# First mixer of a two-model forward pass: projections cut into quarters between the steps of a blocked inverse, level masks on VectorE

## What is computed

```python
u = rms_norm(h, norm_mix[l]); proj = u @ w_in[l]
pool_out = pool_mixer(proj[..., :P], w_pool[l], pool_scale[l])
qkv = causal_conv_silu(proj[..., P:P + 3 * G], conv_w[l])
...
m = einsum('bhncd,bhnjd->bhncj', kb, kh) * decay_strict
sol = triangular_solve(eye(C) + m, [vh * beta, kb * exp(gcum)], lower=True)
...
h = h + concatenate([pool_out, gdn_out]) @ w_out[l]
h = h + square(relu(rms_norm(h, norm_mlp[l]) @ w_up[l])) @ w_down[l]
```

## Time and profile before

| what | us |
|---|---|
| median of the runs | 1176.15 |
| the profiled execution, its own time | 1177.17 |
| its span | 1175.4 |
| TensorE matmul busy | 1098.7 (93%) |
| VectorE / ScalarE / GpSimd busy | 720.2 / 550.3 / 46.5 |
| granted TensorE clock, mean | 0.975 |

### The profile page before, as it was taken

The page is one execution under the profiler, slowest core; times in us unless marked ns, Lnnn a source line. Parts: engine busy times, 40 slices in busy tenths (PEclk is TensorE's granted clock), DMA queues, the critical chain, the costliest instruction groups (busy, mean ns, idle before and its releaser), DMA issues.

```text
span 1175.4 us, 20755 instructions
## 1 busy us (share of the span) xinstructions
PE 1098.7 (93%) x8770; PEld 1064.4 (91%) x8770; DVE 720.2 (61%) x979; ACT 550.3 (47%) x656; POOL 46.5 (4%) x40
## 2 busy tenths in 40 slices
PE   5896688999999999999999999999699999999997
PEld 4886678999999879999999999998589899999997
...
GB/s 294 82 140 108 72 36 72 172 189 178 178 271 196 128 195 179 189 169 179 215 176 181 181 177 126 180 37 158 58 1 1 22 123 150 223 188 188 182 72 36
DMA packets 116960, 167.51 MB, mean 143 GB/s; under 512 B 5792, under 2 KB 97568, under 8 KB 116512
## 3 DMA queue, kind: packets, MB, share of 16 engines
...
...
## 4 chain that ended last, share of the span: by engine, by line
PE 80%; DVE 12%; issue 3%; ACT 3%; DMA 1%; POOL 0%; SPq 0%; DVEq 0%; ACTq 0%; POOLq 0%
PE banks L1874 22%; PE banks L1876 22%; PE banks L1875 22%; DVE sb_w_low L1145 2%; ACT sb_w_high L637 1%; PE banks L2302 1%; PE banks L2379 1%; DVE sb_arena L1215 1%; PE banks L2367 1%; DVE sb_arena L1735 1%; DMA sb_constants<-in_constants 1%; DVE sb_state L1732 1%; PE banks L2010 1%; PE banks L2017 1%; PE banks L2182 1%
## 5 line engine op out<-in xcount | busy, mean ns | idle before, releaser
L1145 DVE TENSOR_TENSOR sb_w_low<-sb_raw,sb_w_high 128x2048 fp32r<-128x2048 f32 x150 | 344.9, 2303 | 274.3 <-ACT sb_w_high L637 274.2
L1874 PE MATMUL banks<-sb_act_high,sb_w_low 128*128 128x256 f32 x1376 | 396.3, 288 | 16.4 <-DVE sb_arena L1204 5.9
L637 ACT ACTIVATE sb_w_high<-sb_raw 128x2048 fp32r<-128x2048 f32 x150 | 285.6, 1910 | 268.4 <-PE banks L1876 268.3
L1876 PE MATMUL banks<-sb_act_high,sb_w_high 128*128 128x256 f32 x1376 | 391.7, 285 | 0.0
L1875 PE MATMUL banks<-sb_act_low,sb_w_high 128*128 128x256 f32 x1376 | 389.1, 283 | 0.0
L1874 PEld LDWEIGHTS banks<-sb_act_high,sb_w_low 128*128 128x128 f32 x1376 | 261.7, 190 | 21.6 <-DVE sb_arena L1204 7.5
L1875 PEld LDWEIGHTS banks<-sb_act_low,sb_w_high 128*128 128x128 f32 x1376 | 264.2, 192 | 0.4 <-issue 0.2
L1876 PEld LDWEIGHTS banks<-sb_act_high,sb_w_high 128*128 128x128 f32 x1376 | 260.8, 190 | 0.0
L1874 PE MATMUL banks<-sb_hidden_high,sb_w_low 128*128 128x256 f32 x896 | 254.2, 284 | 0.6 <-DVE sb_hidden_low L1558 0.6
L1876 PE MATMUL banks<-sb_hidden_high,sb_w_high 128*128 128x256 f32 x896 | 253.5, 283 | 0.0
L1875 PE MATMUL banks<-sb_hidden_low,sb_w_high 128*128 128x256 f32 x896 | 251.3, 280 | 0.0
...
## 6 DMA issues: line engine op xcount, KB each, us to landing
...
```

The lines of the kernel that those rows point to most:

```text
L637: nc.scalar.activation(whi[s][:], raw[s][:], ACT.Copy).then_inc(hi_done, 1)
L1145: nc.vector.tensor_tensor(wlo[s][:], raw[s][:], f32(whi[s][:]), ALU.subtract).then_inc(lo_done, 1)
L1874: nc.tensor.matmul(dst, l_lo, r_hi, start=start, stop=False, **kw)
L1876: return nc.tensor.matmul(dst, l_hi, r_hi, start=False, stop=stop, **kw)
```

## The change

It rewrites the first mixer and leaves the other stages alone, apart from names of masks and semaphore offsets.

- The matrix of ones is set by VectorE; x's semaphore is split in two halves; VectorE squares x (before: ScalarE). The constants are loaded after unit 2 instead of after unit 0 and are smaller.
- Units come in another order: keys, queries, pool columns, values, gate columns. The gates' products move behind unit 1. The keys' convolution, norms and products come early; queries are normalised late.
- The inverse: the 16x16 diagonal blocks are inverted on VectorE by 15 steps of forward substitution, between two 32x32 block transposes; ScalarE gathers the diagonals and spreads the result. Only levels 4, 5 and 6 are left for TensorE. Their masks (`level`) are VectorE's, on whole [128, 1024] tiles into three buffers.
- Units 6 to 9 are cut into quarters (12 matmuls each, `quarter`), which stand between the steps of the levels and of the chunk steps.
- The output projection runs in two halves over k: first the four k of the pool part for all four units, then the four of the delta net.

Cut to its core:

```diff
-LEVELS = 7
+LEVELS = (4, 5, 6)
...
-    IN_COLS = [4, 5, 2, 3, 6, 7, 0, 1, 8, 9]
+
+    IN_COLS = [4, 5, 2, 3, 0, 1, 6, 7, 8, 9]
+
+    CONV_UNITS = [0, 1, 2, 3, 6, 7]
+    OUT_BANKS = [4, 5, 2, 3]
...
         for j, c in enumerate(IN_COLS):
             inner(U_IN + j, w_in_v, c)
-            if j == 0:
+            if j == 2:
                 sp.dma_start(cm[:], dram["constants"]).then_inc(cm_in, 16)
...
-        chain.add(pool.memset(MX.pre[:, :, 0:3], 0.0))
+        pool.memset(MX.pre[:, :, 0:3], 0.0)
+        pool.memset(MX.pre_v[:, :, 0:3], 0.0)
+        pool.memset(MX.pu[:, :, 0:16], 0.0).then_inc(edges_set, 1)
+        chain.add(pool.memset(MX.Wb, 0.0))
+        pool.memset(MX.D, 0.0).then_inc(blocks_set, 1)
+        chain.settle()
+        pool.memset(MX.Wb[:, ::33], 1.0).then_inc(blocks_set, 1)

         pool.wait_ge(cm_in, 16)
         pool.wait_ge(decay_done, 2)
-        pool.tensor_tensor(MX.AT[:], MX.ET[:], cmat("upper").rearrange("p (a b) -> p a b", a=1)
-                           .broadcast_to([P, 8, P]), ALU.mult).then_inc(decay_mask, 1)
-        pool.wait_ge(decay_mask, 1)
-        pool.tensor_tensor(MX.ET[:], MX.ET[:], over(cmat("neg_upper_strict"), 8), ALU.mult)\
-            .then_inc(decay_mask, 1)
-
-        def inversion(call, LT, LTl):
-
-            pool.wait_ge(lt_ready, 2 * call + 2)
-            for l in range(1, LEVELS):
-
-                n = 12 * call + 2 * (l - 1)
-                if n:
-                    pool.wait_ge(inv_x_ps, n)
-                pool.tensor_tensor(LTl[:], LT[:], over(cmat("levels", l), 8), ALU.mult).then_inc(inv_lt, 1)
-
-
-        pool.wait_ge(proj_out, 8)
-        pool.wait_ge(kqn_done, 4)
+        pool.tensor_tensor(MX.AT[:], MX.ET[:], over(cmat("upper"), 8), ALU.mult).then_inc(decay_mask, 1)
+
+        pool.wait_ge(proj_out, 6)
+        pool.wait_ge(gsum_ps, 3)
...
-        inversion(0, MX.LT, MX.LTl)
...
         for k in range(KT):
+            act.wait_ge(x_in[k // 4], 16)
             nc.scalar.activation(act_hi[:, k, :], x[:, k, :], ACT.Copy, scale=vcol("norm_mix", k)).then_inc(a_hi, 1)
-        nc.scalar.activation(MX.sq[:], x[:], ACT.Square).then_inc(sq_done, 1)
+        high(0)
         act.wait_ge(ab_in, 16)
         nc.scalar.activation(wab_hi[:], MX.wab[:], ACT.Copy).then_inc(ab_col, 1)
-        high(0)
+        high(1)
...
+        high(2)
+        first_tap(0)
+        silu(0)
+        high(3)
+        first_tap(1)
+        silu(1)
+        log_exp()
...
+        high(6)
+
+        act.wait_ge(blocks_set, 2)
+        act.wait_ge(lt_ready, 2)
+        for b in range(4):
+            rows = slice(32 * b, 32 * b + 32)
+            last = nc.scalar.activation(in_blocks(MX.D)[rows, :, 0:8].rearrange("p i n -> p n i"),
+                                        MX.LT[rows, :, 32 * b:32 * b + 32], ACT.Copy)
+        last.then_inc(mx_diag, 1)
+        first_tap(3)
+        high(7)
+        high(8)
+        act.wait_ge(mx_base, 1)
+        act.wait_ge(cm_in, 16)
+        for b in range(4):
+            last = nc.scalar.activation(MX.WT[:, :, 32 * b:32 * b + 32],
+                                        in_blocks(MX.E)[:, :, 0:8].rearrange("p i n -> p n i"), ACT.Copy,
+                                        scale=cm[:, CMATS["quads"][0] + b:CMATS["quads"][0] + b + 1])
+        last.then_inc(mx_wide, 1)
+        high(9)
+        take_w(0)
+        silu(2)
+        take_x(0)
+        silu(3)
+        take_w(1)
+        first_tap(4)
+        take_x(1)
+        silu(4)
+        take_w(2)
+        first_tap(5)
+        take_x(2)
...
+        nc.vector.memset(ones, 1.0)
...
+        for h in range(2):
+            hs = slice(4 * h, 4 * h + 4)
+            dve.wait_ge(x_in[h], 16)
+            last = nc.vector.tensor_tensor(MX.sq[:, hs, :], x[:, hs, :], x[:, hs, :], ALU.mult)
+        last.then_inc(sq_done, 1)
...
+        take_pre(0)
+        taps(0)
+        low(3)
+        take_pre(1)
+        taps(1)
...
+        take_pre(2)
+        low(4)
+        taps(2)
+        for m in range(CH):
+            dve.wait_ge(decay_done, m + 1)
+            dve.wait_ge(gsum_ps, m + 1)
+            ms = slice(4 * m, 4 * m + 4)
+            chain.add(nc.vector.tensor_tensor(MX.LT[:, ms, :], MX.ET[:, ms, :], over(cmat("neg_upper_strict"), 4), ALU.mult))
         for m in range(CH):
             dve.wait_ge(prod_ps, m + 1)
+            chain.settle(chain.n - 1 + m)
             for h in range(4):
-                last = nc.vector.scalar_tensor_tensor(MX.LT[:, 4 * m + h, :], bank[2 + m][:, h * P:h * P + P],
-                                                      s[5][:, m, h:h + 1], MX.ET[:, 4 * m + h, :], ALU.mult, ALU.mult)
+                lt = MX.LT[:, 4 * m + h, :]
+                last = nc.vector.scalar_tensor_tensor(lt, bank[2 + m][:, h * P:h * P + P], s[5][:, m, h:h + 1], lt,
+                                                      ALU.mult, ALU.mult)
             last.then_inc(lt_ready, 1)
-        for m in range(CH):
-            dve.wait_ge(prod_ps, 3 + m)
-            at = MX.AT[:, 4 * m:4 * m + 4, :]
-            chain.add(nc.vector.tensor_tensor(at, bank[4 + m][:].rearrange("p (a b) -> p a b", a=4), at, ALU.mult))
-        def inversion_start(call, LT, WT):
-
-            for h in range(2):
-                hs = slice(4 * h, 4 * h + 4)
-                dve.wait_ge(lt_ready, 2 * call + h + 1)
-                chain.add(nc.vector.tensor_tensor(WT[:, hs, :], LT[:, hs, :], over(cmat("levels", 0), 4), ALU.mult))
-                chain.settle()
-                nc.vector.tensor_tensor(WT[:, hs, :], WT[:, hs, :], over(ident, 4), ALU.add).then_inc(inv_wt, 1)
-
-        def inversion(call, WT, meanwhile=lambda l: None):
-
-            for l in range(1, LEVELS):
-                meanwhile(l)
-                for h in range(2):
-                    hs = slice(4 * h, 4 * h + 4)
-                    dve.wait_ge(inv_d_ps, 12 * call + 2 * (l - 1) + h + 1)
-                    dve.wait_ge(inv_wt, 14 * call + 2 * (l - 1) + h + 1)
-                    nc.vector.tensor_tensor(WT[:, hs, :], WT[:, hs, :],
-                                            bank[2 + h][:].rearrange("p (a b) -> p a b", a=4), ALU.add)\
-                        .then_inc(inv_wt, 1)
-
-        inversion_start(0, MX.LT, MX.WT)
-
+        def level(l):
+            nc.vector.tensor_tensor(MX.L[l][:], MX.LT[:], over(level_mask(LEVELS[l]), 8), ALU.mult).then_inc(inv_lt, 1)
+
+        low(5)
+        take_pre(3)
+        low(6)
+
+        dve.wait_ge(kqn_done, 2)
+        dve.wait_ge(lt_ready, 2)
+        level(0)
+
+        dve.wait_ge(mx_diag, 1)
+        chain.add(nc.vector.transpose(MX.B, MX.D))
+        chain.settle()
+        for j in range(15):
+
+            shape = [P, 2, 15 - j, j + 1]
+            tmp = MX.part[:, 0:2 * shape[2] * shape[3]].rearrange("p (s a b) -> p s a b", s=2, b=j + 1)
+            below = MX.W16[:, :, j + 1:16, 0:j + 1]
+            chain.add(nc.vector.tensor_tensor(tmp, MX.B16[:, :, j + 1:16, j:j + 1].broadcast_to(shape),
+                                              MX.W16[:, :, j:j + 1, 0:j + 1].broadcast_to(shape), ALU.mult))
+            chain.settle()
+            chain.add(nc.vector.tensor_tensor(below, below, tmp, ALU.add))
+            chain.settle()
+        nc.vector.transpose(MX.E, MX.Wb).then_inc(mx_base, 1)
+        take_pool(4)
+        dve.wait_ge(mx_base, 1)
+        level(1)
+        take_pool(5)
+        dve.wait_ge(inv_lt, 2)
+        level(2)
+        low(7)
+        taps(3)
+        add_level(0)
+        take_pre(4)
+        low(8)
...
+        add_level(1)
+        taps(4)
+        take_pre(5)
+        taps(5)
+        add_level(2)
+        low(9)
+        normalise(2)
+        normalise(3)
+        take_z(8)
...
+        def quarter(u, b, n):
+
+            s = u % RING
+            h, l = (w[s][:, :].rearrange("p (k n) -> p k n", k=KT) for w in (whi, wlo))
+            if n == 0:
+                pe.wait_ge(lo_done, u + 1)
+            t = n // 2
+            cs = slice(t * P, t * P + P)
+            for k in range(4 * (n % 2), 4 * (n % 2) + 4):
+                ins = split_matmul(bank[b][:, t * T:t * T + T], h[:, k, cs], l[:, k, cs], act_hi[:, k, :],
+                                   act_lo[:, k, :], start=k == 0, stop=k == KT - 1)
+            if n == 3:
+                ins.then_inc(w_used, 1)
+
...
+        take(0)
+        take(1)
         pe.wait_ge(ab_col, 2)
...
+        take(3)
+        take(4)
+        pe.wait_ge(decay_done, 3)
+        for h in range(4):
+            last = nc.tensor.transpose(bank[7][:, h * P:h * P + P], MX.qkv[:, h, 0:P], ident)
+        last.then_inc(tr_ps, 1)
+        take(5)
...
+        part(6, 0)
+        part(6, 1)
+        turn_wt(0)
+        part(6, 2)
+        left_level(0)
+        part(6, 3)
+        right_level(0)
+        part(7, 0)
+        turn_wt(1)
+        part(7, 1)
+        left_level(1)
+        part(7, 2)
+        right_level(1)
+        part(7, 3)
+        turn_wt(2)
+        part(8, 0)
+        left_level(2)
```

(17 more changed lines are left out.)

548 lines of the change are left out of this document (279 added, 269 removed).

## The result

The changed kernel took 1126.22 us (median of 4 runs, 1124.38 to 1127.57), the kernel before 1176.16 beside it: ratio 0.9575, interval 0.9546 to 0.9603. 1130 was forecast, with 1113 to 1150 as range. The profiled execution took 1126.08.

What follows compares the result with a forecast made beforehand. TensorE, busy for 93% of the span, was taken as the bound. Start 9.7, work 131.8, waits 11.8, half-clock 3.0, GpSimd 3.0 and entry 2.1 made 161.4 against 207.8; 1177.2 - 46.4 - 1.0 = 1129.8, predicted 1130, range 1113 to 1150.

Steps and rivals of the forecast that it cites:

- (a): TensorE's wait at unit 0 for its low part, made by ScalarE and VectorE: about 1.0 us.
- (e): TensorE's wait at the first chunk step, 2.2 us, and a last 0.3 before the outputs: 2.5 us.
- work and half-clock loss: TensorE's mixer work at full clock, 131.8 us, plus two spells at the low clock, 1.5 us each: 3.0.
- GpSimd beside VectorE: GpSimd's trailing sums delay VectorE beside low(7), taps(3) and low(8): 3.0 us charged.
- (c): TensorE's wait before quarter 0 of unit 6, for VectorE's pool take behind the whole base inverse: 4.9 us.
- entry of the feed-forward: Behind the output projection, the last pair of k reaches TensorE later than it wants it: 2.1 us.
- (b): TensorE's wait at unit 2, behind the norms of the second pair of keys: about 2, taken as 2.2 us.
- (d): TensorE's waits between level steps: 0.5 us for silu(4) behind taps(4), 0.7 for the norms; together 1.2.
- R4: Rival: inverse not shortened, nine exchanges uncovered by quarters at 0.75 us each, 1137; chance 0.68 together with the forecast.
- R1: Rival: VectorE sets the pace of the mixer's second half, through port, base, copies and clock; about 1147, chance 0.17.
- R3: Rival: TensorE drops to the low clock at the wait of (c) and stays there; up to 1202, chance 0.03.
- R2: Rival: all waits vanish under the quarters, without (b), (d), (e), port cost and entry; 1116, chance 0.10.

Runs made afterwards that it cites:

- the second profile: The changed kernel itself, unaltered, run and profiled again: median 1126.82 us, ratio 0.9577.
- The experiment with the gates' products: Changed kernel with the gates' narrow matmuls put one triple behind each triple of unit 1 instead of all behind it: 1127.14 us, ratio 0.9569.
- all moves together: Changed kernel with both pool takes early, unit 6 whole first, GpSimd's sums and first level mask behind the base inverse, decays' mask on VectorE: 1124.59 us.

## Why the prediction was right, and where it was not

The sum made 161.4; the like in the trace is R plus the growth of what lies behind it: 156.2 + 0.5 = 156.7. Term by term:

| term | forecast | measured |
|---|---|---|
| start | 9.7 | 8.6 |
| waits (a) to (e) | 11.8 | 10.7 (1.0, 0, 6.0, 1.5, 2.2) |
| work and half-clock loss | 131.8 + 3.0 | 136.1, TensorE's busy time in the seven stretches |
| GpSimd beside VectorE | 3.0 | within (c) |
| entry of the feed-forward | 2.1 | 1.3 (0.8 ahead of R, 0.5 behind) |

That the total is so near is in part luck. Most of the mechanisms that were named are in the trace, but their sizes were off both ways: 1.1, 1.1, 3.0 and 0.8 us too much for the start, the waits, GpSimd and the entry, 1.3 too little for work and clock, 4.7 in all. The sum of the waits hides 2.2 too much in (b) and 1.1 too little in (c). And 1.0 of the 4.7 was made up by subtracting that the profiled execution before lay above its median; the one after lay at it (1126.08 against 1126.22).

- **Work and clock.** The clock was at 0.50 from 30.0 to 40.3 us, and from the first matmul of unit 6 (74.15) to 77.8. Half of these 14.0 us of busy time, 7.0, is the most that it can have cost (an estimate), against 3.0; so the work was overestimated by 2.7 at most. The first fall came under the gates' products, ahead of (b) and not behind it. The earlier trace rows have five stretches under 0.95, where the prediction says four, and the earlier trace rows have a DMA share of 0.98 at 27 us, where it says never near 1 behind 25; neither enters the sum.
- **Start.** Sized from x at 8.5 us; x was there earlier (VectorE began to square its second half at 7.20, after a wait for the load), so TensorE began at 8.57. Alone, on the kernel before, the new start brought the first matmul 5.8 us forward and gave 0.5%; 4.7 us (14.4 less 9.7) were summed for it.
- **(a)** 1.05; in the second profile 1.9. Unit 0 began at 15.5 in both.
- **(b)** The chain was right and the cover was mis-sized: with the clock at 0.50 from 30.0 us the gates' products took 7.4 us instead of 5.1, and no wait was left (in the profile with the level masks on GpSimd, where the fall came later, 0.6 us was). Its 2.2 us became half-clock loss. The experiment with the gates' products took the cover away, and 3.4 us of wait appeared.
- **(c)** 4.9 forecast, 6.0 measured, and its cause shown: without the substitution it is gone, with the take moved it stands elsewhere. What was mis-sized is "held 0.8 by GpSimd's mask": the mask met the taps and cost 2.15. Taking 0.29 us for a substitution instruction was right (0.19 to 0.29 by width), and so was the reason, GpSimd asleep. When it isn't, they take 0.6 to 0.7: that case was in the bounds (0.22 to 0.66), and one experiment ran into it. ScalarE's strided copies took 0.70 us (gather) and 0.67 (spread), against 0.5.
- **(d), (e)** 1.5 against 1.2, 2.2 against 2.5.
- **The masks.** "Moved alone they would gain 0" was tested from the other end, in the new order, and there it held. "They cost nothing on the path" is said of the old order, where nothing speaks against it: in the levels each mask ran 2.4 us beside TensorE's products and VectorE's sums, which read PSUM and took 0.69 us each, as always. In the new order they do touch the path. On GpSimd they lengthen VectorE's instructions by 4.2 us and relieve it of 3.6, and the first of them puts E 0.5 later. The Trainium skill (SBUF — State Buffer, Who interferes with whom) has a VectorE instruction with two SBUF inputs and a reading GpSimd instruction exclude each other for a whole instruction; the turns of 0.61 to 0.74 us on both engines agree, and so do the takes from PSUM, which a mask did not lengthen.
- **The 3.0 for GpSimd** was charged for the trailing sums, and these cost nothing that the waits show; the place where GpSimd mattered was its mask, inside (c). The trailing sums lengthened low(7) from 2.3 to 2.7 and the taps from 2.46 to 4.70, but VectorE had slack there (1.15 us idle before the first add).
- **Entry.** 2.1 was too much. TensorE waits 1.2 us in three pieces for low parts of the next activations, two of them (0.8) ahead of R, and the time behind R grew by 0.5.
- **R4** priced nine uncovered exchanges at 0.75. In six that were uncovered, two cost 0.34, one 1.55 by ScalarE's order, and one 0.65 that the changed kernel has too; two cost nothing. So quarters between the levels mattered less by exchange than thought (2.2 us more than in the changed kernel for the six), and the halves of the output projection, which the forecast did not price, were worth 4.1.
- **R1** did not come as a whole, but half of its mechanism is real: from the second key unit to E it is VectorE that sets the pace. What was taken from it there (2.15) or put on it (5.3) moved E by as much. This ends where TensorE becomes the later one: with all moves together, 3 us taken moved nothing.
- **R3** did not come: 78.7 to 156.2 ran at 1.00. **R2** came in part: (b) was gone, and so was the charge for GpSimd, but (d) and (e) stayed at 3.7 and the entry at 1.3. Its five terms also add up to 11.0, not 14; with the half-clock loss of 3.0, which it doesn't name, they would.
